# Feed-forward up projection: one 512-column matmul for high and low token parts, halves added on VectorE

## What is computed

```
def conv_geglu_ffn(hn, w_up, conv_w, conv_b, w_down):
    u = depthwise_conv_centered(hn @ w_up, conv_w, conv_b)
    gate, val = jnp.split(u, 2, axis=-1)
    return (jax.nn.gelu(gate, approximate=True) * val) @ w_down
```

## Time and profile before

| quantity | value |
| --- | --- |
| median of 3 runs | 1020.34 us (1019.22 to 1021.77) |
| span of the profiled execution | 1017.7 us |
| TensorE matmul busy | 96% of the span |
| VectorE, ScalarE, GpSimd busy | 47%, 61%, 68% |
| DMA | 176 GB/s on average |

### The profile page before, as it was taken

The page is one execution under the profiler, slowest core; times in us unless marked ns, Lnnn a source line. Parts: engine busy times, 40 slices in busy tenths (PEclk is TensorE's granted clock), DMA queues, the critical chain, the costliest instruction groups (busy, mean ns, idle before and its releaser), DMA issues. The chain is left out here.

```text
span 1017.7 us, 16075 instructions
## 1 busy us (share of the span) xinstructions
PE 979.9 (96%) x6169; PEld 861.9 (85%) x6169; DVE 477.9 (47%) x993; ACT 622.9 (61%) x1145; POOL 692.8 (68%) x550
## 2 busy tenths in 40 slices
PE   6999998999999898999998899999999999999998
PEld 5898778999999797988877799999978887877887
DVE  3745344444443654876934454444354143223552
ACT  7636557554545775888867565555566577755631
POOL 5977616857577695779778567575778756866573
PEclk9999999999999999999999899999999999999999
DMA  9774425776554555646537455656455745644321
GB/s 334 254 207 155 137 83 176 239 232 202 193 180 135 168 171 164 208 142 230 207 123 232 143 200 174 207 166 207 166 166 175 189 152 179 209 142 133 116 83 42
DMA packets 132234, 178.69 MB, mean 176 GB/s; under 512 B 21489, under 2 KB 94077, under 8 KB 131965
## 3 DMA queue, kind: packets, MB, share of 16 engines
q1 hardware_dynamic: 127981, 169.95, 51.6%
q10 hardware_dynamic: 4176, 7.71, 2.3%
HBM read 176.51 MB, written 5.24 MB: 179 GB/s over the span
## 5 line engine op out<-in xcount | busy, mean ns | idle before, releaser
L521 POOL TENSOR_TENSOR wlo<-raw,whi 128x512 fp32r<-128x512 f32 (+1 forms) x514 | 672.6, 1344 | 295.9 <-ACT whi L1191 280.0
L538 PE MATMUL PS<-Th,whi 128*128 128x256 f32 (+2 forms) x1016 | 290.8, 287 | 3.4 <-DVE Tl L1717 2.8
L539 PE MATMUL PS<-Tl,whi 128*128 128x256 f32 (+2 forms) x1016 | 287.3, 283 | 0.0
L540 PE MATMUL PS<-Th,wlo 128*128 128x256 f32 (+2 forms) x1016 | 287.3, 283 | 0.0
L1191 ACT ACTIVATE whi<-raw 128x1024 fp32r<-128x1024 f32 (+1 forms) x149 | 156.0, 1047 | 165.5 <-PE PS L540 127.7
L535 PE MATMUL PS<-whi,Th 128*128 128x512 f32 (+1 forms) x512 | 203.8, 398 | 6.9 <-DVE Tl L1766 3.3
L1792 DVE SCALAR_TENSOR_TENSOR arena<-PS,cols,arena 128x255 f32<-128x255 f32 (+1 forms) x272 | 118.6, 478 | 193.4 <-ACT arena L1323 166.9
L538 PEld LDWEIGHTS PS<-Th,whi 128*128 128x128 f32 (+2 forms) x1016 | 194.9, 192 | 9.6 <-issue 5.6
L537 PE MATMUL PS<-whi,Tl 128*128 128x512 f32 (+1 forms) x512 | 198.1, 387 | 0.0
L536 PE MATMUL PS<-wlo,Th 128*128 128x512 f32 (+1 forms) x512 | 197.9, 386 | 0.0
L539 PEld LDWEIGHTS PS<-Tl,whi 128*128 128x128 f32 (+2 forms) x1016 | 194.9, 192 | 1.8 <-issue 0.7
(11 more groups left out here) (238 smaller groups left out, 1034.9 us busy)
## 6 DMA issues: line engine op xcount, KB each, us to landing
raw<-in_ffn_w_up_dram SPq DMA_DIRECT2D x44, 1024.0 KB, 5.1
raw<-in_ffn_w_down_dram SPq DMA_DIRECT2D x22, 1024.0 KB, 4.9
raw<-in_w_in_dram SPq DMA_DIRECT2D x22, 1024.0 KB, 5.1
raw<-in_c_w_in_dram SPq DMA_DIRECT2D x16, 1024.0 KB, 5.3
raw<-in_ab_w_in_dram SPq DMA_DIRECT2D x14, 1024.0 KB, 6.7
raw<-in_c_w_out_dram SPq DMA_DIRECT2D x8, 1024.0 KB, 4.9
raw<-in_ab_w_out_dram SPq DMA_DIRECT2D x4, 1024.0 KB, 5.1
raw<-in_c_w_in_dram SPq DMA_DIRECT2D x8, 512.0 KB, 5.4
```

Source lines behind the costliest of these rows:

```text
L521: i = nc.gpsimd.tensor_tensor(wlo[n % NLO][:, c:e], raw[n % NRAW][:, c:e], whi[n % NHI][:, c:e].bitcast(F32), ALU.subtract)
L538: mm(o, wh, ah, start=first, stop=False)
L539: mm(o, wh, al, start=False, stop=False)
L540: return mm(o, wl, ah, start=False, stop=last)
```

## The change

`Th` and `Tl` become the two halves of one tile `T2`. In the feed-forward's G and V slots `slot_split` takes the place of `slot_fm`: for a weight block, one matmul of 512 columns takes the high weights against high and low tokens side by side and writes a whole PSUM bank (left half high by high, right half high by low); a second one of 256 columns adds low weights by high tokens to the right half. So each half m of a slot has a bank of its own, G uses banks 0 and 1 and V banks 2 and 3 in every step.

VectorE then adds the two halves of each bank with a `tensor_reduce` into a new SBUF buffer, `fsm`, and ScalarE's centre tap and VectorE's four taps read `fsm` in place of PSUM.

```
+        T2 = sb("T2", [P, 2, 16, S], F32R)
+        Th, Tl = T2[:, 0], T2[:, 1]
...
+        fsm = [view(3072 + 1024 * i, 4, S) for i in range(2)]
...
+            def slot_split(name, b, fresh=None):
...
+                for m in range(2):
+                    for k in range(KD):
+                        if fresh and m == 0:
+                            pe.wait_ge(*at("T_lo", (fresh, k)))
+                        c = k * 256 + m * P
+                        mm(PS[:, b + m, :].rearrange("p (a s) -> p a s", a=2), h[:, c:c + P], T2[:, :, k, :],
+                           start=k == 0, stop=k == KD - 1)
+                        i = mm(PS[:, b + m, S:2 * S], l[:, c:c + P], Th[:, k, :], start=False, stop=k == KD - 1,
+                               skip_group_check=True)
+                    i.then_inc(*(done("w_used", n) if m else done("f_first", name)))
...
-                        if i >= 2:
-                            pe.wait_ge(*at("f_conv", (l, i - 2)))
-                        slot_fm(("G", l, i), 2 * (i % 2), ("n", 2 * l + 1) if i == 0 else None)
-                        if i == 0:
-                            pe.wait_ge(*at("T_lo", (("n", 2 * l + 1), KD - 1)))
-                        slot_fm(("V", l, i), 2 * (i % 2) + 1)
+                        if i:
+                            pe.wait_ge(*at("f_sum", (l, i - 1, 1)))
+                        slot_split(("G", l, i), 0, ("n", 2 * l + 1) if i == 0 else None)
+                        if i:
+                            pe.wait_ge(*at("f_sum", (l, i - 1, 3)))
+                        slot_split(("V", l, i), 2)
...
+                            act.wait_ge(*at("f_sum", (l, i, q)))
...
-                                           PS[:, 2 * (i % 2) + q // 2, (q % 2) * S:(q % 2 + 1) * S], ACT.Identity,
+                                           fsm[i % 2][:, q, :], ACT.Identity,
...
-                    bank = lambda q: PS[:, 2 * p + q // 2, (q % 2) * S:(q % 2 + 1) * S]
+                    bank = lambda q: fsm[p][:, q, :]
...
+                        for m in range(2):
+                            name = ("GV"[hv], l, i)
+                            dve.wait_ge(*(at("w_used", slot_no[name]) if m else at("f_first", name)))
+                            nc.vector.tensor_reduce(bank(2 * hv + m), PS[:, 2 * hv + m, :].rearrange("p (a s) -> p s a", a=2), AXX,
+                                                    ALU.add).then_inc(*done("f_sum", (l, i, 2 * hv + m)))
```

More of the change, by code:

```diff
@@ L159, in build @@
         hn = sb("hn", [P, NT, D])
-        Th = sb("Th", [P, 16, S], F32R)
-        Tl = sb("Tl", [P, 16, S], F32R)
+        T2 = sb("T2", [P, 2, 16, S], F32R)
+        Th, Tl = T2[:, 0], T2[:, 1]
         aTh = sb("aTh", [P, 2, 2, S], F32R)
@@ L579, in slot_fm @@
                     i.then_inc(*done("w_used", n))
+            def slot_split(name, b, fresh=None):
+                n = slot_no[name]
+                pe.wait_ge(*low(n))
+                h, l = whi[n % NHI], wlo[n % NLO]
+                for m in range(2):
[8 more added lines that the diff above has]
+                    i.then_inc(*(done("w_used", n) if m else done("f_first", name)))
             def slot_dn(name, ah, al, first, b0=4, mid=None, halves=(0, 1)):
```

## The result

The changed kernel takes 1047.9 us (median of 4 runs, 1047.03 to 1049.68) against 1021.06 us for the kernel before (median of 4, 1019.22 to 1033.52; the table above has three of them). The ratio is 1.0264, 95% interval 1.0222 to 1.0307. Three single runs further down (1203 us with short conversions, 1935 us with adjacent halves, 2460 us of the kernel before) were in a slower state and are left out of every median and ratio. The profiled execution has a span of 1045.4 us, 27.7 us more than before.

What follows compares the result with a forecast made beforehand. TensorE was taken to bound the kernel (979.9 of 1017.7 us busy); afterwards VectorE's 17.6 us step would, adding 14.0 us per feed-forward, +28.0: span 1045.7, runs 2.6 above, 1048 us, range 1022 to 1064.

Steps and rivals of the forecast that it cites:

- G(1) to G(9): Eight feed-forward steps with a D slot, each going from 16.98 to 17.6 us: +5.0 us.
- G(9) to G(10): Feed-forward step without a D slot: 14.3 us on VectorE against TensorE's 11.52 us, +2.8 us.
- G(10) to the first transpose: End of a feed-forward: D(10) needs `aTl` of step 10 and waits 7.1 us in place of 0.5, +6.6 us.
- Taps take turns with GpSimd: VectorE's taps, both operands in SBUF, wait out a running GpSimd instruction: about 1.46 us each, against 0.445 as now.
- The ring on VectorE: VectorE's in-order work of one step through ScalarE: 12.5 us without a turn lost, 17.6 with, above TensorE's 16.58.
- the other 5.1 us of GpSimd's work must stand between VectorE's: Of GpSimd's 10.1 us a step, 5.0 fit while VectorE leaves the port free; 5.1 lengthen VectorE's step.
- The wait ahead of D(10): TensorE at the last down slot waits for late `aTl`: 7.1 us in place of 0.5.
- The lower clock: TensorE's clock falling to the lower level after the new waits would add to the loss; no size given.
- TensorE's gain: Feed-forward weight blocks take 0.3475 us instead of 0.360; over 704 blocks 8.8 us are saved.
- turns stay hidden: Rival, chance 0.10: VectorE's step stays under 16.58 us, TensorE sets the beat, 1012 us.
- Sums: VectorE's four reductions from PSUM a step: 0.69 us long, 0.60 us apart, 2.4 us a step, no stride surcharge.
- strided sums cost the double: Rival, chance 0.10: sums over pairs 256 elements apart add 2.4 us to VectorE's step, 1072 to 1096 us.

Runs made afterwards that it cites:

- short conversions: The changed kernel, but GpSimd converts only the first 128 of every 512 columns of the G and V slots; 1026.78 us, ratio 1.0068.
- adjacent halves: High and low part of each token tile side by side in SBUF: 1020.75 us in the kernel with sums in PSUM, 1047.29 us in the changed kernel.

## Why the prediction was right

The forecast was 1048 us, the measured median is 1047.9. The mechanism was the right one and the steps can be checked one by one. The agreement to 0.1 us is luck: several sizes were off and cancelled. In feed-forward 0, read from the starts of the slots, forecast and measured change are:

| stretch | forecast | measured |
| --- | --- | --- |
| G(0) to G(1) | -0.4 | -0.2 |
| G(1) to G(9) | +5.0 | +4.6 |
| G(9) to G(10) | +2.8 | +2.5 |
| G(10) to the first transpose | +6.6 | +7.9 |
| together | +14.0 | +14.8 |

Feed-forward 1 adds 13.0 us, since there the kernel before also lost some time at the lower clock.

- *Taps take turns with GpSimd.* Shown. Back in PSUM, the taps cost 0.48 us again and the loss is gone (1021.05 us); with the old matmuls and taps in SBUF it is there in full (1048.35 us); in SBUF with no GpSimd instruction beside them they cost 0.48 us too.
- *The ring on VectorE.* Forecast 17.6 us, measured 17.74. But the step "the other 5.1 us of GpSimd's work must stand between VectorE's" named the wrong rule. What counts is how many taps find GpSimd running, and how long its instruction is: the ring went to 16.70 and 19.56 us with other pieces for the same work. Eight taps lost 5.11 + 3.16 - 3.56 = 4.7 us, near enough to 5.1 by chance of the piece size. And the ring without turns is 13.0 us, not 12.5: from the first sum to the first tap it is 1.95 us, not 1.7, twice a step. The two errors cancel.
- *The wait ahead of D(10).* Forecast 7.1 us, measured 5.7. The lower clock, which the prediction named only as an addition and left out of its sum, more than made up for it: 1.4 us in slot G(10), and 1.4 us behind D(10)'s start (9.90 us instead of 8.54 to the transpose). That is 2.8 of the 7.9 us of the last stretch.
- *TensorE's gain.* Mis-sized: 0.3535 us for a block instead of 0.3475, 4.6 us instead of 8.8. It had been added up from matmuls in runs of one size, and here the sizes change. Under the ring it hardly counted; in the rival "turns stay hidden" it would have made 1016.6 us (1020.3 - 4.6 + 0.9) and not 1012 us. No run tried that case without other waits.
- *Sums.* 0.68 us each and 0.60 from start to start, pairs 256 elements apart: no surcharge, so the rival "strided sums cost the double" is out. Doubling their number left the step as it was.

## What to carry to other kernels

When a VectorE operand moves from PSUM to SBUF, look at what GpSimd runs beside it: here an instruction with two SBUF operands waited out the GpSimd instruction that was running, so the price is counted in GpSimd instructions and not in VectorE's elements. Short GpSimd pieces made each turn cheaper (3.12 us for four taps instead of 5.11), keeping one operand in PSUM made it free, and so did taps that ran when GpSimd was idle (1.79 us). Before cutting the number of matmuls, measure the distance between their starts: here only the fixed part of each was to be had, and half of that was lost to the change of sizes, so that 4.6 us of 1020 were left. And look behind each new wait: TensorE's clock may be lower there.

## What was not expected of the hardware

- Matmuls of 512 and 256 columns in turn take 0.3535 us a pair, although runs of one size take 0.2275 and 0.120; grouped by size it is 0.348, as the two add up to. The layout of the moving operand, one stretch or two, makes no difference (0.353).
- A tap with both operands in SBUF takes 0.48 us when GpSimd is idle, and up to 0.96, 1.52 and 2.63 us beside GpSimd instructions on 256, 512 and 1024 columns.
- A VectorE reduction over pairs 256 elements apart in a PSUM bank takes 0.68 us for 512 elements, as a contiguous one does.
- The granted clock fell to its lower level around a wait of 2.5 us and again around one of 5.7 us, after TensorE had been busy for 5.01 of 10 us. It cost 1.4 us each time.
